# Moving five pieces in a one-core decoder step: a small matmul, the routing products of a mixture of experts, its table of weights, and two loads ahead of three gathers

## What is computed

```python
def hier_moe(x, rg_w, rg_b, re_w, re_b, w1, w3, w2):
    pg = jax.nn.softmax((t @ rg_w + rg_b).astype(F32), axis=-1)
    pg_top, g_idx = lax.top_k(pg, 1)                      # one group of four
    ...
    e_val, e_idx = lax.top_k(le_sel, TOP_K_IN)            # two experts of that group
    wts = jax.nn.softmax(e_val, axis=-1) * pg_top
    ...
    h = jax.nn.silu(jnp.einsum('nd,edf->nef', t, w1)) * jnp.einsum('nd,edf->nef', t, w3)
    h = h * gate[..., None].astype(h.dtype)
    return jnp.einsum('nef,efd->nd', h, w2).reshape(b, l, d)

def layer(...):
    s = ...                                               # scores of the decoding tokens
    p = jax.nn.softmax(s, axis=-1)                        # over 2049 keys
    ...
    y = hres + hier_moe(rms_norm(hres, p['norm2']), ...)
```

## Time and profile before

| | before |
|---|---|
| median of 3 runs | 841.17 us (839.34 to 841.94) |
| profiled execution, its own time | 840.35 us |
| its span | 838.6 us |
| PE busy | 793.9 us, 95% |
| DVE, ACT, POOL busy | 46%, 27%, 33% |
| mean granted clock of PE | 0.981 |

### The profile page before, as it was taken

How to read it: one execution, slowest core, us unless ns; L and a number is a source line. 1 busy time by engine, 2 the same in 40 slices (tenths; PEclk the granted TensorE clock), 3 DMA queues, 4 the chain that set the end, 5 groups by cost and what they waited for, 6 DMA issues and landing times.

```text
span 838.6 us, 14311 instructions
## 1 busy us (share of the span) xinstructions
PE 793.9 (95%) x5314; PEld 566.9 (68%) x5314; DVE 382.8 (46%) x700; ACT 225.8 (27%) x427; POOL 277.5 (33%) x204
## 2 busy tenths in 40 slices
PE   8999999989999999899999999999999789999991
PEld 7887777666677787677776777888888544333330
DVE  4671676757478588654550411543311632031210
ACT  4222324331423635114224212421201521020110
POOL 0000421244554773236453554523000021242223
PEclk9999999999999999999999999999999989999997
DMA  9243632245555531245443461161156769999943
GB/s 367 90 147 90 214 101 77 76 143 157 163 182 186 165 120 63 77 139 164 147 156 113 156 199 64 64 214 65 51 196 257 286 237 361 391 373 376 384 164 48
DMA packets 72154, 147.23 MB, mean 176 GB/s; under 512 B 13207, under 2 KB 47016, under 8 KB 70036
## 3 DMA queue, kind: packets, MB, share of 16 engines
q1 hardware_dynamic: 65716, 135.43, 46.4%
q0 software_dynamic: 5920, 10.82, 5.1%
q10 hardware_dynamic: 448, 0.06, 0.1%
HBM read 137.71 MB, written 18.90 MB: 187 GB/s over the span
## 4 chain that ended last, share of the span: by engine, by line
PE 76%; DVE 10%; DMA 4%; POOL 3%; SPq 3%; issue 2%; ACT 2%; POOLq 0%; DVEq 0%; ACTq 0%
PE ps L854 21%; PE ps L578 12%; PE ps L1157 7%; PE ps L1061 7%; PE ps L823 6%; PE ps L1226 4%; PE ps L621 3%; PE ps L593 3%; DMA br<-in_w 3%; PE ps L876 2%; PE ps L923 2%; PE ps L653 2%; SPq L484 2%; POOL kv L2420 1%; PE ps L567 1%
## 5 line engine op out<-in xcount | busy, mean ns | idle before, releaser
L578 PE MATMUL ps<-xn,ring 128*128 128x268 f32 (+1 forms) x576 | 140.0, 399 | 1.0 <-ACT qb L1319 0.9
L578 PEld LDWEIGHTS ps<-xn,ring 128*128 128x128 f32 x576 | 109.3, 194 | 26.7 <-issue 3.4
L2420 POOL TENSOR_TENSOR kv<-kv,sgd 128x1024 f32<-128x1024 f32 (+1 forms) x32 | 80.8, 2536 | 121.4 <-DVE tmp L1765 70.2
L1462 ACT ACTIVATE sgt<-sgt,vec 128x260 f32<-128x260 f32 x60 | 30.2, 511 | 142.7 <-DVE sgt L2027 82.9
L2510 POOL DMA_INDIRECT out_y<-cst,gtab x24 | 37.3, 1555 | 79.7 <-DVE cst L2345 38.9
L823 PE MATMUL ps<-br,ring 128*128 128x260 f32 x256 | 61.6, 387 | 0.8 <-DVE sgt L2038 0.8
L854 PE MATMUL ps<-xn,ring 128*128 128x260 f32 x240 | 58.7, 387 | 1.0 <-ACT tmp L1319 1.0
L854 PE MATMUL ps<-xn,qb 128*128 128x260 f32 x240 | 59.1, 390 | 0.0
L1061 PE MATMUL ps<-qk,ring 128*128 128x260 f32 x256 | 56.5, 383 | 0.0
L823 PEld LDWEIGHTS ps<-br,ring 128*128 128x128 f32 x256 | 47.6, 190 | 11.3 <-issue 2.8
L1061 PEld LDWEIGHTS ps<-qk,ring 128*128 128x128 f32 x256 | 48.6, 190 | 7.8 <-issue 0.4
(11 more groups left out here) (474 smaller groups left out, 1448.9 us busy)
## 6 DMA issues: line engine op xcount, KB each, us to landing
ring<-in_w_mg SPq DMA_DIRECT2D x32, 640.0 KB, 4.4
kv<-in_kc SPq DMA_DIRECT2D x128, 128.0 KB, 2.1
kv<-in_vc SPq DMA_DIRECT2D x128, 128.0 KB, 2.1
ring<-in_w_in SPq DMA_DIRECT2D x24, 512.0 KB, 4.6
kv<-in_w SPq DMA_DIRECT2D x8, 1024.0 KB, 14.7
br<-in_w SPq DMA_DIRECT2D x7, 1024.0 KB, 18.6
sgd<-in_w SPq DMA_DIRECT2D x6, 1024.0 KB, 18.5
qk<-in_w SPq DMA_DIRECT2D x6, 1024.0 KB, 14.5
```

The costliest lines, as they stand in the source:

```text
L578: mm = pe.matmul(ps[:, 2 * (t % 2) + h, 0:hw], wsl(c, k), xnv[:, k, col0 + h * hw:col0 + (h + 1) * hw], start=(k == 0), stop=(k == KT - 1))
L1462: act.activation(g, g, ACT.Sigmoid, bias=vv(V_BM + 8 * "ABCD".index(n) + m + i)).then_inc(g_a, 1)
L2420: pool.tensor_tensor(kb, kb, qbc[:, b:b + 1, :].to_broadcast([P, HALF // 2 + (half and u), 256]), ALU.mult)\
```

## The change

Five moves, nothing added or removed:

1. The product of ones with the sums of exponentials (L1014) goes one place earlier in step 3: ahead of the second product of the step and of the first pair block.
2. The rank products go ahead of the first transpose of residual rows; and the five transposes of residual rows all stand behind them, ahead of the products that make the table of token numbers.
3. PE's last transpose for the weights' table (L1136) goes behind the transposes of the first gathered rows. On DVE its copy and sum, and with them `g_ok`, go behind the copy of slot 0.
4. SP's wait for the third gather goes from weights 10 to weights 12, which makes 10 and 11 free to start when the residuals are transposed.
5. The wait of the weights' table for copies by ACT (`tt_a`) asks for all ten.

```diff
@@ SP
             sp.wait_ge(tt_t, 2 * NB)
-            sp.wait_ge(m_xe[ROUNDS - 1], 16)
             weights(10)
             weights(11)
             for b in range(3, NB):
                 residual(b)
             sp.wait_ge(y_out, 16 * NB)
+            sp.wait_ge(m_xe[ROUNDS - 1], 16)
             weights(12)
@@ PE
-                if (p, at) == (3, 2):
+                if (p, at) == (3, 1):
                     pe.wait_ge(*s_sum)
                     pe.matmul(ps[:, 5, 64:128], cc(C_ONE, P), sm, start=True, stop=True).then_inc(s_tot[0], 1)
...
             for b in range(1, NB):
                 rows_of(hgT, b, b)
-            rows_of(hTr, 0, NB)
             pe.wait_ge(sel_ok, 1)
...
-            for b in range(1, 3):
+            for b in range(NB):
                 rows_of(hTr, b, NB + b)
             for b in range(NB):
                 pe.wait_ge(oh_ok, 2 * b + 3)
...
-            rows_of(hTr, 3, NB + 3)
-            rows_of(hTr, 4, NB + 4)
             pe.wait_ge(oh_ok, 2 * NB + 2)
-            pe.wait_ge(tt_a, NB + 3)
+            pe.wait_ge(tt_a, 2 * NB)
...
             mm.then_inc(wts_t[0], 1)
-            pe.wait_ge(sel_ok, 3)
-            pe.transpose(ps[:, 2, P:P + 64], slots[0:64], ident[0:64, 0:64]).then_inc(wts_tt[0], 1)
...
             rows_T(0)
             rows_T(1)
+            pe.wait_ge(sel_ok, 3)
+            pe.transpose(ps[:, 2, P:P + 64], slots[0:64], ident[0:64, 0:64]).then_inc(wts_tt[0], 1)
@@ DVE
-            two_kinds(wts_t, 2)
-            dve.wait_ge(*wts_tt)
-            link(dve.tensor_copy(slots[:, 64:128], ps[:, 2, P:P + 64]))
-            tt(g_w[:, 0:n_t], kinds[0], kinds[1], ALU.add).then_inc(g_ok, 1)
+            dve.wait_ge(*wts_t)
+            dve.tensor_copy(slots[0:64, :], ps[0:64, 2, 0:P]).then_inc(sel_ok, 1)
...
-            for i in range(ROUNDS):
-                rows_copy(i)
+            rows_copy(0)
+            dve.wait_ge(*wts_tt)
+            link(dve.tensor_copy(slots[:, 64:128], ps[:, 2, P:P + 64]))
+            tt(g_w[:, 0:n_t], kinds[0], kinds[1], ALU.add).then_inc(g_ok, 1)
+            rows_copy(1)
+            rows_copy(2)
```

## The result

| | before | after |
|---|---|---|
| median of 9 runs | 839.34 us (836.16 to 841.94) | 842.69 us (841.69 to 844.64) |
| profiled execution, its own time | 840.35 us | 842.57 us |
| its span | 838.6 us | 840.8 us |
| mean granted clock of PE | 0.981 | 0.973 |

What follows compares the result with a forecast made beforehand. PE was taken as the bound, busy 95% of the span, though hardly in the routing. Terms -1.6 - 1.8 + 2.0 + 1.1 + 2.5 - 1.2 = +1.0 us gave a median of 842.2 us, range 836.5 to 845.5.

Steps and rivals of the forecast that it cites:

- Edit 1: Step 3 of the merge: DVE divides sooner, -1.6 us, and no low clock behind the third pair block, -1.8 us.
- the clock's part: Step 3 of the merge: PE's fall to half clock behind the 2.34 us stand goes away, -1.8 us.
- The third rival: Step 3 of the merge: a new clock fall behind the 2.0 us stand at 328, +1.8 us, 844.0 us; chance 0.11.
- Edit 2: Routing: rank products start at once, DVE goes on 1.2 us sooner, indices are out and the gather issued 1.5 us sooner.
- Edit 4, the gather: First gather beside loads 10 and 11: lands 8.2 us after issue, 3.5 us more; +2.0 us with the 1.5 gained.
- the second rival: First gather held up in full: lands after 10.5 us, 844.5 us, decided from a landing of 9.7 us on; chance 0.22.
- The first rival: First gather hardly held up, sharing evenly with the loads: lands after 4.7 to 6.1 us, 836.2 to 838.6 us; chance 0.27.
- Edit 3: Start of the experts: ACT's first copy waits for DVE's weights' table and sum, so the experts start later, +1.1 us.
- The clock at the experts' start: PE stands 6.7 us ahead of the gathered rows, so rows and first products run at the low clock: +2.5 us.
- The end: Last output products: PE's wait for the last load goes, as loads start sooner and PE is later: -1.2 us.
- The sum: Whole kernel: all terms together +1.0 us, 841.35 us profiled and 842.2 us on the median; chance of the forecast 0.40.

Runs made afterwards that it cites:

- sums_only: The kernel before with only the product of the sums of exponentials moved one place earlier: 837.87 us, ratio 0.9986.
- both_back: The changed kernel with the weights' table back ahead of the gathered rows and loads 10 and 11 back behind the third gather: 837.51 us, ratio 0.9964.
- back_and_busy: `both_back` with 12 unneeded identity transposes in each of three PE stands (ahead of both tables and the gathered rows): 836.61 us, ratio 0.9965 to before.
- loads_back: The changed kernel with SP's wait for the third gather back ahead of loads 10 and 11: 838.16 us, ratio 0.9984 to before.
- one_load: The changed kernel with only load 10 ahead of the wait for the third gather, load 11 behind it: 842.97 us, ratio 1.0032 to before.
- loads_only: The kernel before with only SP's wait for the third gather moved behind loads 10 and 11: 840.42 us, ratio 0.9994.
- table_back: The changed kernel with the weights' table back ahead of the gathered rows on PE and DVE: 842.2 us, ratio 1.0043 to before.
- warm_longer: The changed kernel with 44 unneeded identity transposes ahead of the first gathered rows and 12 between rows and first expert products: 839.32 us, ratio 0.9990 to before.
- warm: The changed kernel with 28 unneeded identity transposes ahead of the first gathered rows: 841.53 us, ratio 1.0005 to before.

## Why the prediction was right or wrong

**Edit 1: -3.4 forecast, -3.1 measured.** The third pair block comes 1.4 us sooner where 1.6 was taken, the clock's part is 1.65 where it was 1.8, and the stand ahead of the block is 0.30, under the 0.5 forecast. `sums_only` shows both parts alone. But they hold for one profile of before and one of each new kernel. The third rival, a new fall behind the stand at 328 (1.8 us were said to come back), was not there in after's profile and was there in seven of the eleven profiles with the new order. The time from the step's first product to the first transpose tells the three cases apart: 324.54 to 324.57 us without a fall (after, `sums_only`, `both_back`, `back_and_busy`), 325.8 to 325.9 in five others and 327.4 in two (`loads_back`, `one_load`), so 1.3 or 2.9 us more. The old order has its own falls, behind the 2.34 us stand: 327.64 in before, 330.88 in `loads_only`, whose clock stayed at 0.50 from 344.2 to 354.4:

```profile
343.73 1.73 PE L923 MATMUL ps<-tmp 32*128 32x128 f32 x16 [2.34 <-DVE vtok L1972]
...
349.15 2.08 PE L923 MATMUL ps<-tmp 32*128 32x128 f32 x16
351.16 3.60 PE L823 MATMUL ps<-br,ring 128*128 128x260 f32 x8
```

So the fall in step 3 cost nothing, 1.3 or 2.9 us in the new order. In the two profiles of the old order it cost 1.65 us and 3.2 more than that; neither is without a fall. The runs of `sums_only` and before, 1.8 us apart by the medians and 1.2 by the ratio, are the better price of the edit. The forecast gave this rival 0.11 as a matter of yes or no for the kernel, where each execution comes out its own way.

**Edit 2: -1.5 forecast, -1.1 measured** from the first transpose to the gather's issue. DVE goes on at 658.67 where the forecast had 662.3 less 3.8 for what lay ahead, 658.5. The five blocks took PE's stand, as forecast: 4.53 us without a gap, and 1.56 us of stand left where 1.3 was said. But PE did not keep its full level: the clock fell again at about 665.5 behind that shorter stand, and the first table took 2.23 us. At full level it takes 1.97 (`both_back`, and `back_and_busy`, whose clock was 1.00 throughout), not the second table's 1.53, since its products follow the rows that DVE makes one by one (2.04 us, L2286). `both_back` gained 1.4, nearly the forecast.

**Edit 4, the gather: 8.2 us forecast, 9.5 measured.** This is the step on which the sign hung, and the term that was mis-sized: +3.5 forecast, +4.8 measured. The forecast took 8.2 and not 10.5 because part of the loads would be done by the time of the gather. They were not: SP's queue was still behind with the stores ahead of them, and of the 2.95 MB of loads and stores 2.77 were moved after the gather's issue. The four profiles with both loads and both stores ahead show 8.3 to 9.5, from the forecast up to just under the 9.7 from which the second rival was to decide. The first rival, an even sharing with a landing of 4.7 to 6.1 us, is out: it took for the whole of the delay what is its second part. The rule on arbitration in the Trainium skill (DMA: Bandwidth & Descriptors, in Queues, rings and completion order, not in the section that the prediction names) is that an engine takes turns between its queues. It agrees with after's view of transfers from 676 to 680 us, when both queues had 42 to 45% of the engines. It is not what the start of a gather shows: none of its packets for 2.5 to 5.2 us beside loads, and in `one_load` from 674 to 675 us 14% of the engines against 85% for SP's queue. What passes there no view shows, and that stays open.

**Edit 3: +1.1 forecast, +0.9 measured** by `table_back` in the profile, and ACT's first copy was released by DVE as said. From rows to products 3.70 us instead of 3.0, because the transposes were slow too.

**The clock at the experts' start: +2.5 forecast.** Rows to products and the first products lost 1.8 + 1.7 us together; less 0.9 for edit 3, 2.6. `warm_longer` takes it back in its profile. In `warm`, with 2.66 and 1.56 us of stand left, the products were slow again.

**The end: -1.2 forecast, -1.2 measured.** The wait is gone, but here it needed no moved loads: it is gone in `both_back`, `loads_back` and `sums_only` as well. By these profiles what decides is how far load 10 is ahead of PE. It was issued 0.15 us behind the first expert product in before (681.07, 680.92) and 0.5 behind it in `back_and_busy` (677.86, 677.32), and both wait 1.1 to 1.2 us at the end; in `both_back` it is 0.6 us ahead (678.15, 678.79), with PE another 1.7 later through its clock, and nothing waits. In `sums_only` it is 0.2 behind, and only the slow first products (3.53 us) can have done away with the wait. So in after the slow clock alone would have given the term. With the clock up, `back_and_busy`, without edit 4, waits 1.1 us and `warm_longer`, with it, does not: there the forecast's reason may hold.

**The sum.** +1.0 forecast, +2.2 in the profiles: 1.3 more than said on the gather, 0.4 on the indices and 0.3 on edit 1, nearly nothing from the other terms, and 0.7 less from the stretch ahead of the change. On the medians, +3.4. The one large error is the size of the gather's delay; the second is that the forecast was set on three runs of before whose median lay 1.8 us above that of nine. The two errors cancel in the time (842.2 against 842.69), and that is luck; the places, and the sign of each term, were right.

## What to carry to other kernels

A transfer that a queue may start early is not free because the engines are idle: ask which small transfer on another queue comes next on the critical path, and keep large ones behind it unless the end waits for them by more than that costs. Price PE's stands by what runs behind them at half the clock, and fill the ones just ahead of a critical stretch, with real work or with transposes that nothing needs. In `warm`, filled only in part, they left the products slow; and in `back_and_busy` filled stands gave no time that the ratios show, and the end waited for a load. And compare an edit of under 2 us on the medians of ten runs and more, since one profile shows one draw of the clock.

## What was not expected of the hardware

- A gather on POOL's queue, issued with 2.7 to 2.8 MB of loads and stores still to move on SP's, moved its first packet 3.3 to 5.2 us behind the issue in four profiles (4.7 to 5.2 in after), against 1.7 to 2.3 with nothing or only stores beside it.
- PE's clock fell to 0.50 behind stands of 1.80 us in seven of eleven profiles, and behind one of 1.56 us in after's own routing. In step 3 it was back after 3 to 7 us, and in `loads_only`, behind the stand of 2.34 us, after 10. Kernels with the same program up to there fell in one profile and not in another.
- Transposes of the identity brought PE's level of 2.4 GHz back and held it through a wait for a gather (44 of them took 5.71 us, the first 1.5 us at 0.50), and delayed nothing that the profile shows.
